# Side pieces of a hybrid encoder layer's projection: three beside a merged first stage, nine beside the last scan group, five in attention

## What is computed

```python
h = rmsnorm(x, norm_mix)
proj = h @ w_in
q, k, v, z, xbc, dt_f, dt_b, gate_a, gate_s = split(proj)
attn = window_attention(rope(rmsnorm(q)), rope(rmsnorm(k)), v, attn_sink)
ssm  = gated_norm(bidirectional_scan(silu(conv(xbc)), softplus(dt_f, dt_b)), z)
x = x + (sigmoid(gate_a) * (attn @ w_out_attn) + sigmoid(gate_s) * (ssm @ w_out_ssm)) @ w_o
x = x + hierarchical_moe(rmsnorm(x))
```

## Time and profile before

| | |
|---|---|
| runs of the kernel before | median 2050.53 us of 3 (2049.47 to 2055.22) |
| the profiled execution: its own time | 2054.24 us |
| its span, from the first to the last instruction | 2052.4 us |
| mean granted TensorE clock over the span | 0.940 |
| stages 1 and 2 | 0 to 63.2 us |
| `ssd_groups` | 63.2 to 746.4 us (its last group from about 633) |
| `attention` | 746.4 to 1028.7 us (its loop from about 840) |

### The profile page before, as it was taken

One profiled execution on the slowest core, in us unless ns is written; L12 is line 12 of the kernel. 1 busy time (PEld: TensorE's weight loads), 2 busy tenths in 40 slices (PEclk: granted clock), 3 DMA queues, 4 the chain that ended last, 5 costly groups with the idle time before them and its releaser, 6 DMA issues. The chain is left out here.

```text
span 2052.4 us, 26125 instructions
## 1 busy us (share of the span) xinstructions
PE 1842.6 (90%) x9426; PEld 1420.9 (69%) x9426; DVE 1283.2 (63%) x1351; ACT 1006.8 (49%) x1579; POOL 639.4 (31%) x368
## 2 busy tenths in 40 slices
PE   4898999999999779899999898985999999999991
PEld 3777787787787645677888786444677777777771
DVE  2677866875884835433344354124888888888883
ACT  4244543533444431355675420122577787777761
POOL 5247646746754933100134431000010111111000
PEclk7999999999999978899999999986999999999996
DMA  3243452424335442231155444512899999999985
GB/s 110 66 128 91 118 141 80 129 85 131 109 107 147 134 160 57 70 126 37 44 183 168 145 154 150 229 72 84 302 355 374 372 375 366 378 370 372 375 301 199
DMA packets 228110, 379.50 MB, mean 185 GB/s; under 512 B 14576, under 2 KB 176624, under 8 KB 203312
## 3 DMA queue, kind: packets, MB, share of 16 engines
q1 hardware_dynamic: 220272, 363.45, 51.8%
q0 software_dynamic: 7168, 12.60, 1.8%
q10 hardware_dynamic: 576, 2.18, 0.3%
HBM read 333.94 MB, written 55.25 MB: 190 GB/s over the span
## 5 line engine op out<-in xcount | busy, mean ns | idle before, releaser
L2011 DVE TENSOR_TENSOR e_w_low<-e_raw,e_w_high 128x2048 fp32r<-128x2048 f32 x190 | 426.5, 2286 | 63.3 <-ACT e_w_high L2007 63.3
L523 POOL TENSOR_TENSOR w_w_low<-w_raw,w_w_high 128x1024 fp32r<-128x1024 f32 x92 | 250.4, 2722 | 456.0 <-ACT w_w_high L518 456.0
L2007 ACT ACTIVATE e_w_high<-e_raw 128x2048 fp32r<-128x2048 f32 x190 | 349.9, 1914 | 0.0
L185 PE MATMUL bank<-h_high,w_w_high 128*128 128x512 f32 (+1 forms) x912 | 320.7, 352 | 31.9 <-ACT ssd_conv_in L802 16.7
L185 PE MATMUL bank<-h_low,w_w_high 128*128 128x512 f32 (+1 forms) x912 | 312.2, 342 | 0.0
L185 PE MATMUL bank<-h_high,w_w_low 128*128 128x512 f32 (+1 forms) x912 | 311.7, 342 | 0.0
L185 PEld LDWEIGHTS bank<-h_high,w_w_high 128*128 128x128 f32 x912 | 178.4, 196 | 65.0 <-issue 29.9
L2023 PE MATMUL bank<-e_w_high,e_xT_high 128*96 128x512 f32 x512 | 206.8, 404 | 3.2 <-DVE e_xT_low L2101 1.6
L2023 PE MATMUL bank<-e_w_high,e_xT_low 128*96 128x512 f32 x512 | 203.2, 397 | 0.0
L2023 PE MATMUL bank<-e_w_low,e_xT_high 128*96 128x512 f32 x512 | 202.3, 395 | 0.0
L946 DVE SCALAR_TENSOR_TENSOR ssd_xc<-ssd_conv_in,ssd_conv_p,ssd_xc 128x774 f32<-128x774 f32 x144 | 194.7, 1352 | 10.8
(11 more groups left out here) (282 smaller groups left out, 3582.4 us busy)
## 6 DMA issues: line engine op xcount, KB each, us to landing
e_raw<-in_w_gate SPq DMA_DIRECT2D x64, 1024.0 KB, 7.6
e_raw<-in_w_up SPq DMA_DIRECT2D x64, 1024.0 KB, 7.6
e_raw<-in_w_down SPq DMA_DIRECT2D x64, 1024.0 KB, 6.9
w_raw<-in_w_in SPq DMA_DIRECT2D x68, 512.0 KB, 4.1
ssd_decays<-decay_sums SPq DMA_DIRECT2D x48, 512.0 KB, 6.6
projected<-ssd_side SPq DMA_DIRECT2D x33, 384.0 KB, 2.5
w_raw<-in_w_out_ssm SPq DMA_DIRECT2D x16, 512.0 KB, 4.1
y_ssd<-ssd_y SPq DMA_DIRECT2D x24, 256.0 KB, 2.4
```

What stands on the lines that cost most here:

```text
L185: last = pe.matmul(out, lhs[k][a], rhs[k][b], start=(k == 0 and m == 0), stop=(k == n - 1 and m == 2))
L523: pool.tensor_tensor(self.pair[u].low[:, :, :], self.raw[u][:, :, :], self.pair[u].high[:, :, :].bitcast(F32), ALU.subtract).then_inc(self ...
L2007: act.activation(pair[n].high[:, :], core.raw[c][:, :], ACT.Copy).then_inc(high_ok, 1)
L2011: dve.tensor_tensor(pair[n].low[:, :], core.raw[c][:, :], pair[n].high[:, :].bitcast(F32), ALU.subtract).then_inc(low_ok, 1)
```

## The change

Stages 1 and 2 become one block, `front`. In it:

- three side pieces (FRONT = 3, the first tiles of q) are loaded, split and multiplied; the first sequence's products (`first(n)`) stand on PE after the transposes of tiles 3, 4 and 5, the second sequence's (`second(n)`) between the steps of the step-size chain;
- POOL keeps only the first half of each tile's `h.low`; DVE takes the second half. POOL's queue has `lower_piece(0..2)` at tiles 3, 4, 5, behind that tile's `h.low`;
- the transposes use four banks instead of eight, `scaled` runs two tiles ahead, the step-size product of the first sequence stands behind the transposes of tile 2, and the load and rounding of the three xbc pieces (numbers 3 to 5) are behind the side pieces'.

The last scan group has nine side pieces, one in each time step. Attention has five: 15 units, nine in the opening as before and six in the loop, in every fourth group (groups 3, 7, 11, ...). Four clearing writes of `y_rows` (786 KB each) are issued together. The total of pieces is the same; their order on the ring shifts by three.

```diff
-SIDES, LAST_SIDES = 9, 6
-SSD_SIDES = (SG - 1) * SIDES + LAST_SIDES
+FRONT, SIDES, LAST_SIDES = 3, 9, 9
+SSD_SIDES = FRONT + (SG - 1) * SIDES + LAST_SIDES
...
+            @block.tensor    # in front
+                def steps(s):
+                    if s:
+                        pe.wait_ge(dtT_ok, s)
+                    pe.wait_ge(w_low_ok, 1)
+                    pe.wait_ge(first_low_ok, FIRST[s] + TILES[s])
+                    pe.wait_ge(second_low_ok, FIRST[s] + TILES[s])
+                    products(...).then_inc(dtT_mm, 1)
+                def first(n):
+                    core.pieces.ready(pe, n)
+                    products(pe, core.bank[FIRST_BANK[n]][:, 0:SEQS[0]], ...).then_inc(first_mm, 1)
+                def second(n):
+                    products(pe, core.bank[1 + n][:, 0:SEQS[1]], ...).then_inc(core.pieces.done, 2)
...
+                for t in range(NT):
+                    transposes(t)
+                    if t == 2:
+                        steps(0)
+                    if t > 2:
+                        first(t - 3)
+                steps(1)
+                second(0)
...
+                second(1)
+                pe.wait_ge(a_ok, 1)
...
+                second(2)
...
             def _(pool):
...
-                    for j in range(2):
-                        pool.wait_ge(high_ok, 2 * t + j + 1)
...
+                    pool.wait_ge(high_ok, 2 * t + 1)
...
+                                       ALU.subtract).then_inc(first_low_ok, 1)
+                    if t >= FRONT:
+                        lower_piece(pool, core, t - FRONT)
+                for n in range(FRONT):
+                    lower_piece(pool, core, n + RING)
...
+                def leave_second(n):
+                    core.pieces.finished(act, n, 1)
+                    act.activation(side[n][:, by_sequence(1)], ...).then_inc(second_left, 1)
+                    round_piece(act, core, n + RING)
...
-LAST_STEP_SIDES = ((3,), (4,), (5,), (), (), ())
+LAST_STEP_SIDES = ((3,), (4,), (5,), (6,), (7,), (8,))
...
-    OPENING = len(UNITS) - len(GROUPS)
+    OPENING = 9
+    REST = len(UNITS) - OPENING
+    UNITS_AT = [range(OPENING + g * REST // len(GROUPS), OPENING + (g + 1) * REST // len(GROUPS))
+                for g in range(len(GROUPS))]
...
-                            unit(OPENING + m // QPK)
+                            for u in UNITS_AT[m // QPK]:
+                                unit(u)
```

More of the change, by code:

```diff
@@ L222, in refined_root, with front @@
     return dve.tensor_tensor(out, out, part, ALU.mult)
[L225 removed]
+def front(core):
     nc = core.nc
@@ L252, in _ @@
                 sp.dma_start(core.w_dt[:, :, :], core.w_in_cols(DT0, 2 * SH)).then_inc(core.w_dt_in, 16)
+                for n in range(2 * RING):
+                    load_piece(sp, core, n)
+                for n in range(FRONT):
+                    sp.wait_ge(first_left, n + 1)
+                    sp.wait_ge(second_left, n + 1)
+                    sp.dma_start(core.projected[n * P:(n + 1) * P, :], side[n][:, :]).then_inc(side_out, 16)
+                    if n == FRONT - 2:
+                        sp.wait_ge(sumT_ok, 2)
+                        for d in range(2):
+                            sp.dma_start(core.sums[d], sumT[:, d, :]).then_inc(sumT_out, 16)
@@ L274, in _ @@
                                        ACT.Copy).then_inc(high_ok, 1)
+                    if t == 0:
+                        act.wait_ge(core.w_dt_in, 16)
+                        act.activation(w_pair.high[:, :, :], core.w_dt[:, :, :], ACT.Copy).then_inc(w_high_ok, 1)
+                    if 0 < t <= FRONT:
+                        round_piece(act, core, t - 1)
+                    if t == NT - 2:
+                        step_parts(0)
+                act.activation(rate[:, :], core.row[:, R_ALOG:R_ALOG + H2], ACT.Exp).then_inc(rate_ok, 1)
+                for n in range(FRONT):
+                    leave_first(n)
+                step_parts(1)
+                leave_second(0)
+                act.wait_ge(raw_ok, 1)
+                act.activation(low[:, :, :], low[:, :, :], ACT.Exp)
+                act.drain()
+                act.activation(low[:, :, :], low[:, :, :], ACT.Ln, bias=core.ones[:, 0:1]).then_inc(soft_ok, 1)
+                act.wait_ge(dt_ok, 1)
+                act.activation(tab["log_dt"], tab["log_dt"], ACT.Ln)
+                leave_second(1)
+                act.wait_ge(exp_in_ok, 1)
+                for name in ("reach", "to_end", "decay"):
+                    last = act.activation(tab[name], tab[name], ACT.Exp)
+                last.then_inc(exp_ok, 1)
+                leave_second(2)
             @block.gpsimd
@@ L306, in _ @@
                 dve.wait_ge(core.params_in, 32)
-                scaled(0)
+                for t in range(2):
+                    scaled(t)
                 for t in range(NT):
-                    if t + 1 < NT:
-                        scaled(t + 1)
                     for j in range(2):
@@ L318, in _ @@
                                           gain.unsqueeze(2).to_broadcast([P, 4, P]), ALU.mult).then_inc(gained, 1)
[L320 to L334, removed]
@@ L337, in step_sizes @@
[L337 to L425, removed]
-                for u in range(RING):
-                    lower_piece(pool, core, u)
-            @block.vector
-            def _(dve):
-                dve.wait_ge(w_high_ok, 1)
-                dve.tensor_tensor(w_pair.low[:, :, :], core.w_dt[:, :, :], w_pair.high[:, :, :].bitcast(F32),
-                                  ALU.subtract).then_inc(w_low_ok, 1)
@@ L703, in scan @@
                     store(g, NT - 1)
-                for n in range(RING, GC + 2 * RING):
+                for n in range(2 * RING, FRONT + GC + 2 * RING):
                     load_piece(sp, core, n)
@@ L789, in _ @@
                 pe.sem_inc(y_mm, NT)
-                for n in range(GC):
+                for n in range(FRONT, FRONT + GC):
                     project(n, n % RING)
@@ L1118, in _ @@
                                 sp.dma_start(core.k_both[half * HD:(half + 1) * HD, kv, :], k).then_inc(k_copied, 16)
-                    if 2 <= i < 2 + D // ZW:
-                        zeros(i - 2)
+                    if i == 2:
+                        for c in range(D // ZW):
+                            zeros(c)
                 for u in range(2):
```

156 lines of the change are left out of this document (121 added, 35 removed).

## The result

The changed kernel takes 2063.59 us (median of 6 runs, 2059.7 to 2065.21) beside 2052.4 us for the kernel before (6 runs, 2049.47 to 2055.22): a ratio of 1.0054, 95% interval 1.0041 to 1.0067. It is slower by some 11 us, where 8 us less had been forecast. Its profiled execution took 2059.7 us (span 2057.7, clock 0.944), the lowest of the six, and that of before 2054.24 (span 2052.4); so the two traces show 5.3 of the 11 us. The other 6 lie between single executions of the same kernel, and no trace shows where.

A forecast was written before the change was run, and what follows sets the result against it. PE was taken to bound attention's loop, with room in the front and last scan group. -38.7 + 4.3 + 26.1 = -8.3 us, giving 2045.9 for the profiled execution and 2042.2 against the median; range 2032 to 2057.

The forecast's parts named there:

- The front, +26.1: Front: with three side pieces moved in, the first xbc piece starts at 89.4 instead of 63.26 us, +26.1.
- the ring: Front, from tile 3 on: transposes, POOL's two low parts, `first` and the next transposes wait in turn, 10.8 us a lap.
- The last group, +4.3: Last scan group: of three added pieces one is free in idle time, two go on PE's path, +4.3 us.
- Attention, -38.7: Attention's loop: 18 fewer units save 53.1 us, stalls they covered give back 14.4, so -38.7 us.
- the weakest end that was put to it (-31): Attention's loop: with a stall of 1.2 us the saving is 31 us.
- the prediction's own signs of being wrong: Attention's loop: a clock under 0.95, or ACT as the releaser of the transposes.
- Rival (a): Attention's loop: the clock falls in each run of three groups with no unit, +40 us, so 2082; chance 0.13.
- (b): Front: laps of 9.2 us and the sums at their half, 7 us less, 2035; chance 0.20.
- (c): Attention's loop: ACT's copies and exponentials bind a group at 6.7 us, saving 21, time 2060; chance 0.12.
- (d): Whole kernel: side pieces are left out or done twice; the counts say no, and no chance was given.

The follow-up runs named there:

- second trace: The changed kernel run again unaltered, for another trace and time: 2062.66 us, ratio 1.0068.
- three edits: The changed kernel with first-sequence products behind all six transposes, loop units in groups 0, 4, 8 and so on, last y store ahead of the load: 2041.53 us.

## Why the prediction was wrong

For the profiled executions the sum said 2045.9 us, and the trace gave 2059.7: 13.8 us more. The table's rows give 1.0 for the front, 6.1 for the scan, 12.5 for the loop, -1.6 for the opening and -4.3 for the unchanged stages, 13.7 together. The other 7.6 us of the miss lie between the profiled executions and the medians (3.7 for before, 3.9 for after).

- **The front, +26.1: right.** Laps of 10.5 us (forecast 10.8), idle for half of it, the first xbc piece at 90.33 (forecast 89.4); the kernel with the transposes first showed that the ring is the cause (75.33). The forecast saw that the front gives nothing back beyond the pieces' own price; the remaining gain hung on the other two terms.
- **The last group, +4.3: right as far as it went.** +4.6 to the last product's end; POOL's three low parts (2.35 to 3.37 us) were covered, but for 0.7 us ahead of each of two steps in the second trace. The step that failed is the end: the sum stopped at the last product, and the +3.1 us behind it were put at nothing. The ninth piece moved a load onto SP's queue right ahead of the stage's last store; half of the 3.1 us is that store (1.6, by the run with the store ahead). Another 0.7 is DVE's last row beside POOL's low part of the ninth piece, as the traces have it; no run took that part away. The last 0.8 stays open, and so do the 2.7 us ahead of t = 2, which are within the spread of traces.
- **Attention, -38.7: this step failed.** The loop gave -26.2, beyond the weakest end that was put to it (-31). Of the missing 12.5, 8.8 are the clock (the loop's head, 33.1 against 24.3 us with a unit in group 0), and the other 3.7 are in the main stalls priced too low: the pitch from pair to pair is 1.33 us as forecast (1.4), but the second pair takes 1.04 us instead of 0.65, because each of its two heads waits in turn for DVE's reading. Units were priced as work only; the unit of group 0 was also what ended a low clock. Rows 8 had shown that the loop begins at the low level, and rows 2 that it is high in the mean (0.99); that something had to bring it back in between was not asked. One of the prediction's own signs of being wrong came: the clock over the whole loop is 0.91, under 0.95.
- **Rival (a) named the mechanism and misplaced it.** It had the clock fall in every run of three groups with no unit, at +40 us. Behind the unit of group 3 it never fell inside the loop, with stalls of 0.76 us at most; it only failed to rise at the head, at +8.8. The Trainium skill (TensorE: Matmul & The Clock Gate, "Part 1: The HAM clock gate") lets the clock fall after idle time, and for the loop the trace agrees: 3.67 us of it stood before the loop, and the short stalls inside brought nothing down. For the opening idle time says less: the clock fell there behind 1.23 us of it (in the changed kernel at 823.7, when PE had been busy again for 2.3 us), and once more near 861, when the last idle time had been 0.67 us. The same section lets activity raise the clock again, and by PE's busy time alone this does not fit: 28.5 of 31.0 us busy at 0.51 here, 17.17 of 17.20 at 0.50 in the opening. What decides it, no run here tells: the rotations of the opening ran at 0.50 for 17 us in one trace and brought the clock back after 3.4 us in another.
- **Rivals (b) and (c)** did not come about: the laps were 10.4 and 10.5, and the waits in the loop were for DVE's reading of scores (10.2 us behind group 3), not ACT's copies. As for (d), PE has the same 9426 instructions as before.
- **The chances.** Terms of 26 and 39 us of opposite sign left 8 us, and the error of the larger one alone was more than that. The range ended at 2057, although the three terms' own worst ends, +9 us, come to 2059.5 and the full rival (a) to 2082. In the event all three terms missed on the same side, by 1.0, 6.1 and 12.5.

## What to carry to other kernels

Filler work on PE can do two jobs, filling idle time and bringing the clock back; before it is moved, look in the windows for the granted clock at the place it leaves, and where that is low leave one dense unit (at the loop's head one such line was worth 8 us; in the opening a second one came with 5 us less, not clear of noise). Work put into an idle stage fills nothing if its place on an in-order queue closes a ring of waits through two engines: put it behind the last link that others wait for. And count a stage to its last store, with what now stands ahead of that store on its queue.

## What was not expected of the hardware

- A low clock outlasted dense busy time: PE ran 17.17 of 17.20 us at 0.50 on products of 20 and 128 rows by 256 columns, and about 30 us on scores, transposes and products of 64 columns, until a unit came. It is no rule: in three traces the same rotations brought it back with no unit, after 3.4 us in the changed kernel's second trace and after 6.8 with the store ahead of the load.
- A store of 256 KB issued 0.55 us behind a load of 512 KB on the same queue held the stage's end to 5.3 us after its issue; ahead of the load it was 3.8, and 3.0 in the kernel before, with no load there.
- The same three edits gave 27 us one by one and 21 together. The low stretch at the opening's rotations lasted 20 us in one trace (804.3 to 824.8 with all three edits), 14 in another (823.7 to 837.4 in the changed kernel) and 3.4 in the changed kernel's second, in the same code, and the opening with it 92.3, 87.4 and 82.6 us. So a difference of a few us between single traces, or between kernels that shift the start of attention, need not be the edit's.
